# First layer's third branch as block-product pairs, in a one-core fp32 two-block network

## The chip, the core and the metric

The kernel runs on one core of a Trainium2 chip, everything in fp32. The metric is the device time of one execution in microseconds. TensorE (PE) multiplies, VectorE (DVE) and ScalarE (ACT) work on its results, SyncE (SP) issues the loads of weights, GpSimd (POOL) does little here.

## The reference, cut to what matters

A first block (RWKV-7 and S5 mixers, a convolutional feed-forward) is followed by a second block of two layers of width 1024. In its first layer (l = 0) 512 tokens are computed, 256 of the sequence and 256 of a context; in the second (l = 1) 256. In each layer three branches are gated and summed:

```
parts = split(h @ w_in + b_in)
y_a, yc_a = _gla_mixer(...)            # gated linear attention
y_b, yc_b = _mla_mixer(...)            # 8 softmax heads over 512 keys, then @ mla_wo
# third branch
h = a * sigmoid(g)                     # from parts[9]
h = depthwise_conv(h, 31 taps)
h = silu(layer_norm(h, g, b))
y_c = h @ conv_wo
# merge
g_a, g_b, g_c = split(sigmoid(parts[10]), 3)
y = (g_a * y_a + g_b * y_b + g_c * y_c) @ w_out
x = layer_norm(DN_ALPHA * x + gate1 * y); then a convolutional feed-forward
```

## The kernel before, in words

Features lie on the 128 partitions and tokens along the free axis, so a projection to 128 output features is a *job*: 8 matmuls (128x128 weights, 512 or 256 token columns) into one PSUM bank. Each fp32 matmul stands in the trace as two records. The order of the work is written out by hand: each engine has its own function per stage (`t_` TensorE, `a_` ScalarE, `v_` VectorE), its instructions run in the order written, and named steps (semaphores) tie the engines together. So whatever an engine waits for holds back all that is written behind it.

**Pairs.** `t_pair` (line 724; its matmuls are recorded on line 618) computes two output blocks at once, a 2x2 by 2x2 block product in seven products instead of eight (Winograd's form). Each product is 4 matmuls over half the token columns, 28 matmuls for a pair, in the order P1, P5, P6, a, P7, c, b. Around it VectorE makes four sums of weight blocks ahead (`v_block_sums` through `pair_sums`, lines 631 to 636: S1 is needed by P5, S2 by P6, S3 by P7, S4 by c), and four sums of the input, once for an input (`v_turns`, lines 771 to 776). ScalarE copies P1, P5, P6 and P7 out of PSUM (`a_pair_part`, line 790); P6 may start only when P1 has been copied, P7 when P6 has, c when P5 has, b when P7 has. A copy also waits until VectorE has read the same part of the pair before (the part of P1 is read by its step C11). VectorE adds the parts up (`v_pair_parts`, lines 802 and 808: C11, C22, C12).

**Weights.** All weights are streamed in one order, that of TensorE's use, in slabs of 8 tiles (512 KB, issued on line 4378) through a ring of 6 slabs. Slab s is loaded once slab s-6 is released. A job over 8 tiles releases its slab when its last matmul is done; a pair takes two slabs and releases both only at its end; a piece of the modulation (`more_ada`, line 1812, 8 matmuls with 32 of the tiles) takes four slabs and releases all four at its end.

**The first layer's third branch** (`t_branch_c`, `a_branch_c`, `v_branch_c`, `v_ln`): on TensorE two gate jobs, a piece of the modulation, the mean of the convolution's norm (line 3613), three gate jobs, the variance (line 3627), three gate jobs, two output jobs, and then three pairs `("cp", 0, m)` for the other six outputs. ScalarE takes the sigmoid of each gate straight out of PSUM (line 3603), the squares (3634), the root (3646, 3648) and the silu (3600); VectorE centres (3655), adds up the squares (3640), normalises (3664), sums the input for the pairs, and multiplies and adds the outputs into `Y`. The second branch before it (`t_branch_1`) is made of seven pairs already, the output projection after it (`t_wout`) of two jobs and three pairs.

**The attention's heads** (`t_mla`, `a_mla`, `v_mla`): per head and tile of 128 queries, scores (3329, 3330), maximum on VectorE (3346, 3348), exponential on ScalarE (3356), then ScalarE divides by the sum (`a_mla_norm`: logarithm 3364, exponential 3366, multiplication 3368), TensorE transposes two tiles later (3374), VectorE or ScalarE copies the result (3395, 3386), and TensorE multiplies by the values (3405). VectorE does the convolution's taps (3571) in between. Two gates of the second branch are computed inside the last head, and ScalarE takes their sigmoid (2896) there, with a load of its function table before and one back after it.

Of the kernel before, what the change touches and what calls it, by code (L numbers as in the profile page):

```python
# [17 lines left out]
P = 128  # L18
# [6 lines left out]
D = 1024  # L25
DT = D // P
TX = 256
# [225 lines left out]
def build(nc, t_in, out, known):  # L253
# [3 lines left out]
    with ctx:  # L257
# [271 lines left out]
        mo_tmp = area(mla_at + 11264, 1, 2, 512)[:, 0]  # L529
        assert s5_top <= total - 1024, (rw_top, s5_top)  # L530
# [2407 lines left out]
        def v_branch_1(l, n, done):  # L2938
# [38 lines left out]

        def v_branch_c(l, n):

            g, hn = mix_pairs[l], n // 2  # L2980
# [5 lines left out]
            for i, m in enumerate((2, 4, 6)):  # L2986
                pair_sums(g, i + 1)
                key = ("cp", l, m)

                def gated(e, c):  # L2990
                    cols = slice(c * hn, (c + 1) * hn)
                    ve.wait_ge(vector_steps, V.n)
                    ve.tensor_tensor(gct[:, e, cols], gct[:, e, cols], gtc[:, m + e, cols], ALU.mult).then_inc(vector_steps, V.step())

                v_pair_parts(g, key, lambda e, c: gct[:, e, c * hn:(c + 1) * hn], then=gated)
                ve.wait_ge(vector_steps, V.n)
                ve.tensor_tensor(Y[:, m, 0:n], Y[:, m, 0:n], gct[:, 0, 0:n], ALU.add).then_inc(vector_steps, V.step(("Y", l, 2, m)))
                ve.wait_ge(tensor_jobs, at(("job", (key, "b"))))
                ve.tensor_tensor(gct[:, 1, 0:hn], bank((key, "b"))[:, 0:hn], gtc[:, m + 1, 0:hn], ALU.mult).then_inc(vector_steps, V.step(("free", (key, "b"))))
                ve.wait_ge(vector_steps, V.n)  # L3000
                ve.tensor_tensor(Y[:, m + 1, 0:n], Y[:, m + 1, 0:n], gct[:, 1, 0:n], ALU.add).then_inc(vector_steps, V.step(("Y", l, 2, m + 1)))
# [367 lines left out]

        def t_mla_pt(l, n, hd, qt, k0):  # L3370
            pe.wait_ge(scalar_steps, at(("pn", l, hd, qt)))
# [112 lines left out]
        def v_mla(l, n):  # L3484
# [104 lines left out]

        def a_branch_c(l, n):  # L3590
            act.wait_ge(vector_steps, at(("free", ("br2", l, 1, DT - 1))))
# [566 lines left out]
        def _(tensor):  # L4158
# [39 lines left out]
            for l in range(LAYERS):  # L4198
# [13 lines left out]
                t_branch_c(l, n)  # L4212
# [8 lines left out]
        def _(scalar):  # L4221
# [25 lines left out]
            for l in range(LAYERS):  # L4247
# [18 lines left out]
                a_branch_c(l, n)  # L4266
# [10 lines left out]
        def _(vector):  # L4277
# [40 lines left out]
            for l in range(LAYERS):  # L4318
# [15 lines left out]
                v_ln(("cl", l), acc, n)  # L4334
                v_branch_c(l, n)
# [145 lines left out]
```

## Time and profile before

| | |
|---|---|
| median of 3 runs | 2681.27 us (2681.12 to 2682.8) |
| the profiled execution | 2679.76 us, of which the span of the trace is 2677.6 us |
| TensorE busy | 2622.1 us of the span |
| VectorE, ScalarE, GpSimd busy | 1825.7, 842.1, 86.1 us |
| mean granted TensorE clock | 0.995 |
| weights and inputs read | 309.81 MB, 116 GB/s over the span |

The profile is one execution; busy time counts records, start to end. In a timeline a row joins records of one line that follow each other. The span of the trace leaves 2.2 us of the execution's own time outside.

### The profile page before, as it was taken

The numbers are of one execution on the slowest core, as the hardware profiler recorded it, in microseconds if no ns is written. First come the engines' busy times: TensorE is split into PE (matmuls) and PEld (weight loads), VectorE is DVE, ScalarE is ACT, GpSimd is POOL, SyncE is SP. The second block draws the span as 40 slices with busy tenths as digits, with TensorE's granted clock in tenths as the row PEclk, the third lists the DMA queues.
The fourth block names the chain that finished last, engine by engine and source line by source line (L and its number), as shares of the span: only waits on it lengthen the run. The fifth ranks groups of instructions, "written<-read, shape, count | busy, mean of one in ns | idle before, by whom it ended". The sixth has DMA issues, their size and how long they took to land. (4 is left out here: it accounts for less than half of the span.)

```text
span 2677.6 us, 43472 instructions
## 1 busy us (share of the span) xinstructions
PE 2622.1 (98%) x17092; PEld 2191.1 (82%) x17092; DVE 1825.7 (68%) x3710; ACT 842.1 (31%) x1881; POOL 86.1 (3%) x115
## 2 busy tenths in 40 slices
PE   9999999999999999999999999999999999999998
PEld 8777799978776887668667888888798986798997
DVE  7882399644787477897647766644466557668997
ACT  2033143042543112552122423200454224333431
POOL 0000000001221000000000000000011000000000
PEclk9999999999999999999999999999999999999999
DMA  5553644433332222212322222222321441244443
GB/s 209 181 190 123 218 157 167 174 115 106 116 134 71 95 79 87 71 63 73 117 78 91 98 79 95 79 95 95 116 79 49 150 133 58 94 150 142 160 172 126
DMA packets 86776, 313.66 MB, mean 117 GB/s; under 512 B 9472, under 2 KB 11520, under 8 KB 86320
## 3 DMA queue, kind: packets, MB, share of 16 engines
q1 hardware_dynamic: 85072, 304.25, 32.5%
q0 software_dynamic: 1504, 6.64, 0.7%
q8 instruction: 138, 2.26, 0.3%
q14 instruction: 62, 0.51, 0.1%
HBM read 309.81 MB, written 1.05 MB: 116 GB/s over the span
## 5 line engine op out<-in xcount | busy, mean ns | idle before, releaser
L618 PE MATMUL ps<-sb 128*128 128x128 f32 (+1 forms) x8064 | 1292.9, 323 | 5.9 <-ACT sb L694 3.3
L618 PEld LDWEIGHTS ps<-sb 128*128 128x128 f32 x8064 | 1191.6, 191 | 108.9 <-issue 6.0
L921 PE MATMUL ps<-sb 128*128 128x256 f32 (+1 forms) x2480 | 681.6, 432 | 10.6 <-DVE sb L1000 3.5
L921 PEld LDWEIGHTS ps<-sb 128*128 128x128 f32 x2480 | 469.3, 190 | 207.8 <-issue 139.3
L3571 DVE SCALAR_TENSOR_TENSOR sb<-sb 128x512 f32<-128x512 f32 (+1 forms) x480 | 275.5, 615 | 8.7
L631 DVE TENSOR_TENSOR sb<-sb 128x512 f32<-128x512 f32 x155 | 106.3, 686 | 126.6 <-PE ps L618 85.6
L790 ACT COPY sb<-ps 128x256 f32<-128x256 f32 (+1 forms) x201 | 69.1, 344 | 391.9 <-PE ps L618 319.6
L694 ACT COPY sb<-ps 128x128 f32<-128x128 f32 (+1 forms) x252 | 75.3, 299 | 217.9 <-PE ps L618 213.0
L4142 DVE SCALAR_TENSOR_TENSOR sb<-sb 128x512 f32<-128x512 f32 (+1 forms) x176 | 101.0, 615 | 14.9 <-ACT sb L4088 9.9
L633 DVE TENSOR_TENSOR sb<-sb 128x512 f32<-128x512 f32 x155 | 107.2, 692 | 5.3
L808 DVE TENSOR_TENSOR sb<-sb,ps 128x256 f32<-128x256 f32 (+1 forms) x108 | 41.4, 384 | 98.6 <-PE ps L618 68.9
L636 DVE TENSOR_TENSOR sb<-sb 128x512 f32<-128x512 f32 x155 | 105.9, 683 | 0.0
L634 DVE TENSOR_TENSOR sb<-sb 128x512 f32<-128x512 f32 x155 | 105.9, 683 | 0.0
L727 PE MATMUL ps<-sb 128*128 128x128 f32 x896 | 100.7, 275 | 0.0
L727 PEld LDWEIGHTS ps<-sb 128*128 128x128 f32 x896 | 100.6, 192 | 0.1
L3753 ACT ACTIVATE sb<-sb 128x256 f32<-128x256 f32 (+1 forms) x28 | 12.8, 507 | 166.4 <-DVE sb L3830 152.0
L802 DVE TENSOR_TENSOR sb<-sb 128x256 f32<-128x256 f32 (+1 forms) x56 | 21.8, 390 | 51.3 <-ACT sb L790 43.2
L1812 PE MATMUL ps<-sb 128*32 128x512 f32 x384 | 51.7, 607 | 4.6 <-DMA sb<-in_w 4.6
L4088 ACT ACTIVATE sb<-sb 128x512 f32<-128x512 f32 (+1 forms) x84 | 54.9, 702 | 0.2
L2674 POOL TENSOR_TENSOR sb<-sb 128x256 f32<-128x256 f32 x56 | 47.7, 890 | 215.0 <-ACT sb L2602 215.0
L1000 DVE SCALAR_TENSOR_TENSOR sb<-sb 128x256 f32<-128x256 f32 x32 | 14.0, 479 | 48.8 <-ACT sb L982 38.2
L3346 DVE TENSOR_REDUCE sb<-ps 128x1 f32<-128x512 f32 (+1 forms) x48 | 28.7, 598 | 26.1 <-PE ps L3330 25.9
(518 smaller groups left out, 2761.9 us busy)
## 6 DMA issues: line engine op xcount, KB each, us to landing
sb<-in_w SPq DMA_DIRECT2D x574, 512.0 KB, 3.8
sb<-in_two POOLq DMA_DIRECT2D x2, 1088.0 KB, 7.3
sb<-in_x SPq DMA_DIRECT2D x2, 512.0 KB, 4.8
sb<-in_ctx POOLq DMA_DIRECT2D x1, 1024.0 KB, 9.7
sb<-in_v_bias POOLq DMA_DIRECT2D x2, 512.0 KB, 4.0
sb<-in_par SPq DMA_DIRECT2D x1, 764.0 KB, 6.6
sb<-in_s5b POOLq DMA_DIRECT2D x1, 512.0 KB, 7.9
sb<-in_s5c POOLq DMA_DIRECT2D x1, 512.0 KB, 9.9
```

What stands on the lines that cost most here:

```text
L618: ins = pe.matmul(o, w, xs(i), start=(fresh and i == 0), stop=(i == len(ws) - 1), skip_group_check=True)
L631: ve.tensor_tensor(buf[:, 0], half(s2, 0), half(s2, 1), ALU.add).then_inc(vector_steps, V.step(("S1", key)))
L633: ve.tensor_tensor(buf[:, 1], buf[:, 0], half(s1, 0), ALU.subtract).then_inc(vector_steps, V.step(("S2", key)))
L634: ve.tensor_tensor(half(s2, 0), half(s1, 0), half(s2, 0), ALU.subtract).then_inc(vector_steps, V.step(("S3", key)))
L636: ve.tensor_tensor(buf[:, 2], half(s1, 1), buf[:, 1], ALU.subtract).then_inc(vector_steps, V.step(("S4", key)))
L694: act.copy(f.part[:, i, :], bank((key, bk))[:, 0:f.hn]).then_inc(scalar_steps, A.step((name, key)))
L727: ins = pe.matmul(o[:, tt * P:(tt + 1) * P], xs(i)[:, tt * P:(tt + 1) * P], w, start=(fresh and i == 0 and tt == 0), stop=(i == len(ws) - ...
L790: act.copy(dst, src).then_inc(scalar_steps, A.step((name, key)))
L921: ins = pe.matmul(o[:, i * n:(i + 1) * n], w, rhs(k), start=(k == 0), stop=(k == kt - 1))
L3571: ve.scalar_tensor_tensor(out=o_, in0=s_, scalar=pc(("conv_dw", l, j), m + e), in1=o_, op0=ALU.mult, op1=ALU.add).then_inc(vector_steps, V ...
L4088: act.activation(zb2[e][:, g, 0:n].rearrange("p (a b) -> p a b", b=TX), z2[e][:, g, 0:c, 1:TX + 1], ACT.Identity, bias=pc(("ffn_db", l), g ...
L4142: ve.scalar_tensor_tensor(out=o_, in0=z2[e][:, g, 0:c, j:j + TX], scalar=pc(("ffn_dw", l, j), g * FT + m), in1=o_, op0=ALU.mult, op1=ALU.a ...
```

## The change

In the first layer the third branch's eight gates become four pairs (`cg_pairs`, on the same input sums as the second branch's gates), and its first two outputs become a pair, so that the branch is eight pairs. The mean of the norm stands behind the first of them, the variance behind the second, the piece of the modulation between the third and the fourth. Gates are written to SBUF without their sigmoid, which ScalarE takes later. In the heads, the two gates' sigmoids are put behind the divisions of the last head in both layers, and in the second layer the division moves from ScalarE to VectorE (a reciprocal and a multiplication), without the explicit table load ahead of the heads. The core of the diff:

```diff
+        cg_pairs = Pairs(TX, [area(mla_at + 12800 + i * 1536, 3, 4, P) for i in range(2)], parts_at(mla_at + 15872, TX),
+                         [("cg", 0, m) for m in (0, 2, 4, 6)] + [("cp", 0, 0)])
...
                 pair_sums(g, i + 1)
+                if i == len(g.seq) - 1:
+                    pair_sums(cg_pairs, 0)
...
+        def v_cg_parts(l, n, m):
+            hn = n // 2
+            v_pair_parts(cg_pairs, ("cg", l, m), lambda e, c: gtc[:, m + e, c * hn:(c + 1) * hn])
+
+        def v_branch_c_first(l, n):
+
+            tag, last = ("cl", l), cg_pairs.seq[-1]
+            pair_sums(cg_pairs, 1)
+            v_cg_parts(l, n, 0)
+            ve.wait_ge(tensor_jobs, at(("job", (tag, "mean"))))
+            for k in range(DT):
+                ve.scalar_tensor_tensor(out=acc(k)[:, 0:n], in0=bank((tag, "mean"))[:, 0:n], scalar=-1.0 / D, in1=acc(k)[:, 0:n],
+                                        op0=ALU.mult, op1=ALU.add).then_inc(vector_steps, V.step((tag, "cen", k)))
+            table[("free", (tag, "mean"))] = table[(tag, "cen", DT - 1)]
+            for k in range(1, DT):
+                ve.wait_ge(scalar_steps, at((tag, "sq", k)))
+                ve.wait_ge(vector_steps, V.n)
+                ve.tensor_tensor(lnS[:, 0:n], lnS[:, 0:n], cl_squares[k], ALU.add).then_inc(vector_steps, V.step((tag, "sqsum")))
+            pair_sums(cg_pairs, 2)
+            v_cg_parts(l, n, 2)
+            pair_sums(cg_pairs, 3)
+            ve.wait_ge(scalar_steps, at((tag, "rs")))
+            for k in range(DT):
+                ve.tensor_tensor(acc(k)[:, 0:n], acc(k)[:, 0:n], lnS[:, 0:n], ALU.mult).then_inc(vector_steps, V.step((tag, "nrm", k)))
+            v_cg_parts(l, n, 4)
+            pair_sums(cg_pairs, 4)
+            for k in range(DT):
+                ve.wait_ge(scalar_steps, at(("csilu", l, k)))
+            v_turns(conv_src[l])
+            v_cg_parts(l, n, 6)
+            ve.wait_ge(tensor_jobs, at(("job", (("cg", l, 6), "b"))))
+            pair_sums(mix_pairs[l], 0)
+            v_conv_pair(l, n, cg_pairs, 0)
+            for i, m in enumerate((2, 4, 6)):
+                pair_sums(mix_pairs[l], i + 1)
...
+        def v_mla_norm(l, n, hd, qt, k0):
+            s = spare_of(n, hd, qt)
+            ve.wait_ge(scalar_steps, at(("ex", l, hd, qt)))
+            ve.reciprocal(smx[:, s, 3:4], smx[:, s, 2:3]).then_inc(vector_steps, V.step())
+            ve.wait_ge(vector_steps, V.n)
+            ve.tensor_scalar(pr[s][:, k0:512], pr[s][:, k0:512], smx[:, s, 3:4], None, ALU.mult).then_inc(vector_steps, V.step(("pn", l, hd, qt)))
+
         def t_mla_pt(l, n, hd, qt, k0):
-            pe.wait_ge(scalar_steps, at(("pn", l, hd, qt)))
+            pe.wait_ge(*step_of(("pn", l, hd, qt)))
...
         def a_mla(l, n):
             (a_mla_in_first if l == 0 else a_mla_in)(l, n)
             parts = dict(qn=a_mla_qn, kn=a_mla_kn, vh=a_mla_vh, qr=a_mla_qr, qrs=lambda *x: None)
-            both_tables()
+            if l == 0:
+                both_tables()
...
                     old = later(n, hd, qt, 2)
                     if hd < MH:
                         a_mla_exp(l, n, hd, qt, k0)
-                    if (hd, qt) in gates_at(n):
-                        a_gate(l, n, 1, gates_at(n).index((hd, qt)), gtm)
-                        if hd < MH:
-                            both_tables()
                     if old is not None:
                         a_mla_pt(l, n, *old, qtiles(n)[old[1]][1])
-                    if hd < MH:
+                    if hd < MH and l == 0:
                         a_mla_norm(l, n, hd, qt, k0)
+                    if (hd, qt) == (MH - 1, n // P - 1):
+                        a_gate(l, n, 1, 0, gtm)
+                    if (hd, qt) == (MH, 1):
+                        a_gate(l, n, 1, 1, gtm)
...
+                    old = later(n, hd, qt, 1)
+                    if l and old is not None:
+                        v_mla_norm(l, n, *old, qtiles(n)[old[1]][1])
...
+        def t_branch_c_first(l, n):
+
+            for key in cg_pairs.seq:
+                kind, _, m = key
+                if kind == "cp":
+                    t_pair(cg_pairs, key, conv_src[l], "conv_wo_2", l, 0, P, ready=("csilu", l, DT - 1), first=True)
+                    continue
+                if m == 6:
+                    more_ada()
+                c = IN0["gate"] + 2 * D + m * P
+                t_pair(cg_pairs, key, head_src, "w_in_2", l, c, c + P)
+                if m == 0:
+                    t_ln_mean(("cl", l), n)
+                if m == 2:
+                    t_ln_var(("cl", l), n)
+            for m in (2, 4, 6):
+                t_pair(mix_pairs[l], ("cp", l, m), conv_src[l], "conv_wo_2", l, m * P, (m + 1) * P)
+
         def t_branch_c(l, n):
 
             for m in range(DT):
                 if m == 2:
-                    if l == 0:
-                        more_ada()
                     t_ln_mean(("cl", l), n)
...
+        def a_cg_parts(l, m, parts):
+            for i in parts:
+                a_pair_part(cg_pairs, ("cg", l, m), i)
+
+        def a_cg_close(l, n, m):
+            key = ("cg", l, m)
+            act.wait_ge(tensor_jobs, at(("job", (key, "b"))))
+            act.copy(gtc[:, m + 1, 0:n // 2], bank((key, "b"))[:, 0:n // 2]).then_inc(scalar_steps, A.step(("free", (key, "b"))))
...
+        def a_cl_silu(l, n, ks):
+            for k in ks:
+                act.wait_ge(vector_steps, at((("cl", l), "nrm", k)))
...
+        def a_branch_c_first(l, n):
+
+            tag, last = ("cl", l), cg_pairs.seq[-1]
+            a_cg_parts(l, 0, range(4))
+            a_cg_close(l, n, 0)
+            a_cl_squares(tag, (0, 1))
+            a_cg_parts(l, 2, (0,))
+            a_cl_squares(tag, (2, 3, 4))
+            a_cg_parts(l, 2, (1,))
+            a_cl_squares(tag, (5, 6, 7))
+            a_cg_parts(l, 2, (2, 3))
+            a_cg_close(l, n, 2)
+            a_ln_rs(tag, n)
+            a_cg_parts(l, 4, range(4))
+            a_cg_close(l, n, 4)
+            a_cl_silu(l, n, range(4))
+            a_cg_parts(l, 6, (0,))
+            a_cl_silu(l, n, (4, 5))
+            a_cg_parts(l, 6, (1,))
+            a_cl_silu(l, n, (6, 7))
+            a_cg_parts(l, 6, (2, 3))
+            a_cg_close(l, n, 6)
+            a_cg_sigmoid(l, n, (0,))
+            a_pair_part(cg_pairs, last, 0)
...
+            a_cg_sigmoid(l, n, (6, 7))
+            for m in (2, 4, 6):
+                for i in range(4):
+                    a_pair_part(mix_pairs[l], ("cp", l, m), i)
+
         def a_branch_c(l, n):
-            act.wait_ge(vector_steps, at(("free", ("br2", l, 1, DT - 1))))
...
-                v_ln(("cl", l), acc, n)
-                v_branch_c(l, n)
+                if l == 0:
+                    v_branch_c_first(l, n)
+                else:
+                    v_ln(("cl", l), acc, n)
+                    v_branch_c(l, n)
```

The former body of the loop in `v_branch_c` is now the function `v_conv_pair`, which for l = 0 also waits for the gate's sigmoid.

## Rows read from the trace of the kernel before

**Rows 1.** The page, part 1: busy time, share of the span, instructions.

```profile
PE 2622.1 (98%) x17092; PEld 2191.1 (82%) x17092; DVE 1825.7 (68%) x3710; ACT 842.1 (31%) x1881; POOL 86.1 (3%) x115
```

**Rows 2.** PE timeline, first layer's third branch: start us, us, instructions, xrecords.

```profile
1304.83 13.90 PE L921 MATMUL ps<-sb 128*128 128x512 f32 x32
1318.66 1.92 PE L1812 MATMUL ps<-sb 128*32 128x512 f32 x16
1320.51 1.12 PE L3613 MATMUL ps<-sb 128*128 128x512 f32 x2
1321.47 20.76 PE L921 MATMUL ps<-sb 128*128 128x512 f32 x48
1342.08 1.02 PE L3627 MATMUL ps<-sb 128*128 128x512 f32 x2
1342.93 34.50 PE L921 MATMUL ps<-sb 128*128 128x512 f32 x80
1377.27 36.42 PE L618 MATMUL ps<-sb 128*128 128x256 f32 x168
1413.53 13.90 PE L921 MATMUL ps<-sb 128*128 128x512 f32 x32
```

**Rows 3.** DVE timeline of the same stretch; in brackets the idle time before.

```profile
1321.75 2.48 DVE L3655 SCALAR_TENSOR_TENSOR sb<-ps,sb 128x512 f32<-128x512 f32 x4 [10.39 <-PE ps L3613]
...
1345.66 4.90 DVE L3664 TENSOR_TENSOR sb<-sb 128x512 f32<-128x512 f32 x8 [7.49 <-ACT sb L3648]
1364.84 0.42 DVE L771 TENSOR_TENSOR sb<-sb 128x256 f32<-128x256 f32 x1 [14.28 <-ACT sb L3600]
...
1370.70 0.68 DVE L631 TENSOR_TENSOR sb<-sb 128x512 f32<-128x512 f32 x1
...
1373.23 0.68 DVE L3011 TENSOR_TENSOR sb<-ps,sb 128x512 f32<-128x512 f32 x1
...
1384.44 0.42 DVE L808 TENSOR_TENSOR sb<-sb,ps 128x256 f32<-128x256 f32 x1 [2.84 <-PE ps L618]
...
1406.42 0.69 DVE L631 TENSOR_TENSOR sb<-sb 128x512 f32<-128x512 f32 x1 [3.63 <-DMA sb<-in_w]
```

**Rows 4.** ACT timeline of the same stretch.

```profile
1358.87 5.74 ACT L3600 ACTIVATE sb<-sb 128x512 f32<-128x512 f32 x8
...
1379.19 0.37 ACT L790 COPY sb<-ps 128x256 f32<-128x256 f32 x1 [12.58 <-PE ps L618]
```

**Rows 5.** Three windows: us, busy us (xrecords) by engine, PEclk, DMA share, GB/s.

```profile
2447.10:2450.15 3.05, 0.00 (x2) 0.03 (x1) 2.58 (x8) 1.56 (x4) 0.00 (x0) 1.00 0.00 1
2450.15:2454.10 3.95, 3.95 (x11) 3.18 (x12) 3.38 (x18) 3.68 (x7) 0.00 (x0) 0.57 0.00 0
1205.00:1210.00 5.00, 4.52 (x22) 3.85 (x23) 2.06 (x7) 3.50 (x11) 0.00 (x0) 1.00 0.01 3
```

**Rows 6.** PE timeline, then ACT timeline: end of the first layer's heads.

```profile
1202.95 0.60 PE L3374 MATMUL ps<-sb 128*128 128x128 f32 x4
1205.48 2.83 PE L3405 MATMUL ps<-sb 128*128 128x256 f32 x12 [1.92 <-DVE sb L3571]
...
1201.71 1.28 ACT L2896 ACT_TABLE_LOAD   x1
...
1205.00 0.37 ACT L3386 COPY sb<-ps 128x256 f32<-128x256 f32 x1
```

**Rows 7.** PE timeline, then ACT timeline: start of the second layer's heads.

```profile
2222.67 1.95 PE L3277 MATMUL ps<-sb 128*128 128x128 f32 x16
2225.19 1.12 PE L3329 MATMUL ps<-sb 128*128 128x512 f32 x2 [0.57 <-ACT sb L3300]
...
2224.57 0.57 ACT L3300 COPY sb<-ps 128x512 f32<-128x512 f32 x1
```

**Rows 8.** Window of two heads of the second layer; DVE timeline, multiplication by a scalar.

```profile
2230.03:2253.53 23.50, 23.50 (x110) 16.66 (x109) 18.94 (x42) 8.22 (x23) 0.00 (x0) 1.00 0.17 54
...
1420.23 2.77 DVE L3826 TENSOR_SCALAR sb<-sb 128x512 f32<-128x512 f32 x8
```

More of the change, by code:

```diff
@@ L529, in build @@
         mo_tmp = area(mla_at + 11264, 1, 2, 512)[:, 0]
+        cg_pairs = Pairs(TX, [area(mla_at + 12800 + i * 1536, 3, 4, P) for i in range(2)], parts_at(mla_at + 15872, TX),
+                         [("cg", 0, m) for m in (0, 2, 4, 6)] + [("cp", 0, 0)])
+        cl_squares = [lnS, lnq[:, 0], lnq[:, 1]] + [sb[:, mla_at + 4096 + i * 512:mla_at + 4608 + i * 512] for i in range(4)] + [gtc[:, DT - 1]]
         assert s5_top <= total - 1024, (rw_top, s5_top)
@@ L2976, in v_some_taps @@
             return min(done + more, 4 * CW)
+        def v_cg_parts(l, n, m):
[31 more added lines that the diff above has]
+                pair_sums(mix_pairs[l], i + 1)
+                v_conv_pair(l, n, mix_pairs[l], m)
@@ new lines, in v_conv_pair, with gated @@
+        def v_conv_pair(l, n, g, m):
+            key, hn = ("cp", l, m), n // 2
+            def gated(e, c):
+                cols = slice(c * hn, (c + 1) * hn)
+                if l == 0:
+                    ve.wait_ge(scalar_steps, at(("gates2", l, m + e)))
+                ve.wait_ge(vector_steps, V.n)
+                ve.tensor_tensor(gct[:, e, cols], gct[:, e, cols], gtc[:, m + e, cols], ALU.mult).then_inc(vector_steps, V.step())
+            v_pair_parts(g, key, lambda e, c: gct[:, e, c * hn:(c + 1) * hn], then=gated)
+            ve.wait_ge(vector_steps, V.n)
+            ve.tensor_tensor(Y[:, m, 0:n], Y[:, m, 0:n], gct[:, 0, 0:n], ALU.add).then_inc(vector_steps, V.step(("Y", l, 2, m)))
+            ve.wait_ge(tensor_jobs, at(("job", (key, "b"))))
+            ve.tensor_tensor(gct[:, 1, 0:hn], bank((key, "b"))[:, 0:hn], gtc[:, m + 1, 0:hn], ALU.mult).then_inc(vector_steps, V.step(("free", (key, "b"))))
+            ve.wait_ge(vector_steps, V.n)
+            ve.tensor_tensor(Y[:, m + 1, 0:n], Y[:, m + 1, 0:n], gct[:, 1, 0:n], ALU.add).then_inc(vector_steps, V.step(("Y", l, 2, m + 1)))
@@ L2978, in v_branch_c @@
         def v_branch_c(l, n):
-            g, hn = mix_pairs[l], n // 2
+            g = mix_pairs[l]
             for k in range(DT):
@@ L2987, in v_branch_c @@
                 pair_sums(g, i + 1)
[L2988 to L3001, printed above, removed]
+                v_conv_pair(l, n, g, m)
         def v_branch(l, n, b, gbuf, tbuf, stop=DT):
@@ L3368, in a_mla_norm @@
             act.activation(pr[s][:, k0:512], pr[s][:, k0:512], ACT.Identity, scale=smx[:, s, 3:4]).then_inc(scalar_steps, A.step(("pn", l, hd, qt)))
+        def v_mla_norm(l, n, hd, qt, k0):
+            s = spare_of(n, hd, qt)
+            ve.wait_ge(scalar_steps, at(("ex", l, hd, qt)))
+            ve.reciprocal(smx[:, s, 3:4], smx[:, s, 2:3]).then_inc(vector_steps, V.step())
+            ve.wait_ge(vector_steps, V.n)
+            ve.tensor_scalar(pr[s][:, k0:512], pr[s][:, k0:512], smx[:, s, 3:4], None, ALU.mult).then_inc(vector_steps, V.step(("pn", l, hd, qt)))
         def t_mla_pt(l, n, hd, qt, k0):
-            pe.wait_ge(scalar_steps, at(("pn", l, hd, qt)))
+            pe.wait_ge(*step_of(("pn", l, hd, qt)))
             o = open_job(("pt", l, hd, qt))
@@ new lines, in a_cl_squares @@
+        def a_cl_squares(tag, ks):
+            for k in ks:
+                act.wait_ge(vector_steps, at((tag, "cen", k)))
+                act.activation(cl_squares[k], acc(k), ACT.Square).then_inc(scalar_steps, A.step((tag, "sq", k)))
+        def a_cl_silu(l, n, ks):
+            for k in ks:
+                act.wait_ge(vector_steps, at((("cl", l), "nrm", k)))
+                act.activation(acc(k)[:, 0:n], acc(k)[:, 0:n], ACT.Silu, bias=pc(("conv_ln_b", l), k),
+                               scale=pc(("conv_ln_g", l), k)).then_inc(scalar_steps, A.step(("csilu", l, k)))
@@ new lines, in a_cg_sigmoid @@
+        def a_cg_sigmoid(l, n, ms):
+            for m in ms:
+                act.wait_ge(vector_steps, at(("C12", ("cg", l, m - m % 2))))
+                act.activation(gtc[:, m, 0:n], gtc[:, m, 0:n], ACT.Sigmoid, bias=pc(("b_in", l, "gate"), 2 * DT + m)).then_inc(scalar_steps, A.step(("gates2", l, m)))
+        def a_branch_c_first(l, n):
[21 more added lines that the diff above has]
+            a_pair_part(cg_pairs, last, 0)
+            a_cg_sigmoid(l, n, (1, 2))
+            a_pair_part(cg_pairs, last, 1)
+            a_cg_sigmoid(l, n, (3,))
+            a_pair_part(cg_pairs, last, 2)
+            a_cg_sigmoid(l, n, (4, 5))
+            a_pair_part(cg_pairs, last, 3)
+            a_cg_sigmoid(l, n, (6, 7))
+            for m in (2, 4, 6):
+                for i in range(4):
+                    a_pair_part(mix_pairs[l], ("cp", l, m), i)
@@ L4211, in _ @@
                     t_branch(l, n, 1, "mla_wo_2", lambda k: mO[:, k, 0:n], ahead=GATES_AHEAD)
-                t_branch_c(l, n)
+                (t_branch_c_first if l == 0 else t_branch_c)(l, n)
                 t_wout(l, n)
@@ L4265, in _ @@
                     a_branch(l, n, 1, gtm, first=2)
-                a_branch_c(l, n)
+                (a_branch_c_first if l == 0 else a_branch_c)(l, n)
                 for m in (2, 4, 6):
@@ L4333, in _ @@
                     v_ln_sum(("cl", l), acc, n, k)
-                v_ln(("cl", l), acc, n)
-                v_branch_c(l, n)
+                if l == 0:
+                    v_branch_c_first(l, n)
+                else:
+                    v_ln(("cl", l), acc, n)
+                    v_branch_c(l, n)
                 v_ln_close(l, n, "wo2", 2, ("l1", l), ("ln1_g", l), ("ln1_b", l), (l, 1))
```

## The prediction

> **What bounds the kernel now.** First the page's busy times: TensorE is busy for 98% of the span [rows 1], so time is to be had from its records or from its few waits. Then TensorE's timeline of the branch: from the first gate job at 1304.83 to the end of the last pair at 1413.53 one row starts where the last one ends, 108.70 us without a wait, and no row has a bracket of idle time [rows 2]. VectorE's and ScalarE's timelines of the same stretch show what stands behind each wait: VectorE was idle for 7.49 us before its normalisation and 14.28 us before the input sums [rows 3]. So here only TensorE's amount of work counts, until another engine is late. Last come the heads, where TensorE does wait for ScalarE [rows 6, 7].
>
> **TensorE's work.** The three pairs took 1413.53 - 1377.27 = 36.26 us, 12.09 each, 0.432 per matmul of 256 columns [rows 2]. Ten jobs become five pairs. The jobs took 1318.66 - 1304.83 = 13.83 (two), 1342.08 - 1321.47 = 20.61 (three) and 1377.27 - 1342.93 = 34.34 (five), together 68.78. Five pairs are 60.43. That is **-8.35 us**, all on the path. Modulation (1320.51 - 1318.66 = 1.85), mean and variance are the same work elsewhere. Ten slabs stay ten slabs.
>
> **What the other engines add.** VectorE gets five times four weight sums, 2.53 a pair (from the first 631 row at 1370.70 to 1373.23) [rows 3], and the adding up. That is some 18 us on top of 51 busy in 108.7 us; the sum fits, only the order can hurt. I went through the order, putting the pairs at 12.09. First pair (0 to 12.09): the sums for the second pair and the parts of the first are done before the mean is. Mean at 12.1: centring eight times at 0.6 (four took 2.48), then seven sums of squares at about 0.7, each behind the one before (the 512-column records) [rows 3], end about 11 us later; the variance is due at 25.0 and is ready at 23.3. Root: ready two microseconds before the third pair needs ScalarE. No stall up to the end of the third pair, which I call E.
>
> **The stall.** Between third and fourth pair stands the modulation, moved here with its four slabs. The fourth pair's two slabs are the fifth and sixth behind the third pair's end, so in a ring of 6 they take the places of exactly the third pair's two slabs, released at E and not before. The trace has that case: the pair ending at 1377.27 + 24.17 = 1401.44 releases two slabs, and the weight sums that need them start at 1406.42 behind a wait for DMA: 4.98 us [rows 3]. There it cost nothing, as the pair was due only 12 us later. Here TensorE is due after 1.85. And behind the fourth pair's weight sums VectorE has queued the whole normalisation and the third pair's parts; behind these ScalarE has the silus and the copy of the fourth pair's P1 (it waits for C11 of the third). So from E: slabs 4.98; weight sums 2.53 to 7.51; eight multiplications, 4.83 start to start (4.90 took the row) to 12.34 [rows 3]; C11 0.42 [rows 3]; hand over 0.09; copy 0.37 [rows 4]; hand over 0.11 (the two hand-overs from neighbouring ends and starts in these timelines): **13.33**. P6 would have started at 1.85 + 8 matmuls of 0.432 = 5.30. Stall **+8.03 us**, in two pieces: some 2 us for the first slab and S1, then 5.8 us idle before P6. After P6 nothing is late: ScalarE's four silus left, 0.72 each (eight in 5.74 [rows 4]), and two copies take 3.9 us, as long as P6 and the next product. The input sums of the convolution, 5.86 us (1364.84 to 1370.70) [rows 3], end 22.2 behind E, and the fifth pair wants them at 23.7. From there all runs as before. If the landing is 1 us longer or shorter, so is the stall.
>
> **The clock.** Before the record at 2450.15 TensorE had been idle for 3.05 us; in the 3.95 us behind it the granted clock is 0.57, full and half clock (2.4 and 1.2 GHz) mixed: 0.43 x 3.95 = 1.7 us lost. Behind an idle piece of 1.92 us it is 1.00 [rows 5, 6]. 5.8 us idle is longer than either. Bounds: zero (as behind the shorter wait) and 3.4 (the stretch at half clock twice as long); a gain is excluded. I take the nearest row, **+1.7**. The Trainium skill (TensorE: Matmul & The Clock Gate, Part 1) says that the half clock is the default and activity releases it, so that a long wait is followed by a full cold stretch each time; by that the cost leans to the upper bound. No row has an idle piece as long in mid-work to show it.
>
> **The heads, first layer.** Sigmoid of the first gate, with a table load before it and another behind (1201.71 to 1205.00), delays the copy at 1205.00, for which TensorE waits 1.92 us at 1205.48 [rows 6]. Put behind the last division, the sigmoid leaves the copy free right after the transposes, well before TensorE asks. What is late next is the gate's own bank, wanted about 1214, its sigmoid then done about 1211.5. **-1.9**.
>
> **The heads, second layer.** TensorE waits 0.57 us at 2225.19 for a copy that ScalarE reaches at 2224.57 [rows 7] behind three division steps, 1.1 us of which go to VectorE. **-0.6**. The table load that was explicit now comes by itself ahead of the first exponential, while ScalarE waits. VectorE gets 16 times a reciprocal of one column and a multiplication over 512: the latter between 0.42 (the row of eight at 1420.23, whose records are that long) [rows 8] and 0.69 (a 512-column tensor operation [rows 3]), the reciprocal by the one-column ScalarE steps some 0.2; I take 0.75 together. Two heads have 18.94 busy of 23.50 us [rows 8]; four times 0.75 makes 21.9. Cost nothing, covered by the matmuls; if the cover is gone, up to 0.75 x 16 = 12 us.
>
> **Sum:** -8.35 + 8.03 + 1.7 - 1.9 - 0.6 = -1.1 us on the profiled execution of 2679.76, so 2678.6; the median stands 1.5 above that execution, so **2680.1 us**. No change that a measurement can tell: that takes about 0.2%, 5.4 us.
>
> **Rivals.**
> 1. *The wait is covered.* The slabs come in time, or VectorE is not held by them. Then 2681.27 - 8.35 - 2.5 = 2670.4; with TensorE waiting only for landing and S1 (2.2 us), 2672.6. For it: the branch shows no wait before, and the modulation is easy to misplace by a slab. Against it: ring arithmetic and the 4.98 us [rows 3]. Chance 0.15.
> 2. *Half clock twice as long*, by the idle piece of 5.8 us: 2680.1 + 1.7 = 2681.8. The Trainium skill's page above leans this way. Chance 0.17.
> 3. *Slower: VectorE becomes the bound in the second layer's heads.* Place: 16 divisions queued ahead of the taps, each also waiting for the exponential. Two heads leave 4.56 us, 1.14 a division [rows 8]; beyond that every further 0.5 us costs 8. At 1.64 us: 2680.1 + 0.6 + 8 = 2688.7. Against it: the prices above, half of that. Chance 0.06.
> 4. *The change saves no TensorE time*, 28 small matmuls costing what 16 wide ones do: 2680.1 + 8.35 = 2688.5. Against it: the three pairs measured beside it [rows 2]. Chance 0.02.
>
> The forecast itself has 0.60. Its own range: favourable ends (no clock loss, landing 1 us shorter) 2677.4, the others (clock 3.4, landing longer, heads give nothing) 2685.3. To leave out no more than 2 in 10 I go from 2674.5 to 2684.5. Faster by over 0.2% is rival 1: 0.15, plus 0.01 of a much shorter stall, 0.16; slower 3 and 4, 0.08; the rest, 0.76, within.
>
> **What would show it.** The branch's TensorE rows: eight pairs of 12.1 us; up to E no bracket; behind the modulation an idle piece of about 2 us (DMA or line 631), then one of about 5.8 before the third product of the fourth pair, put down to ScalarE's copy; VectorE idle some 13 us before the sums (line 631) of the fourth pair, waiting for in_w; PEclk below 1 behind it. At the first layer's last head the 1.92 us gone. It would be wrong if no such wait shows and the branch takes 100 us, or if the second layer's heads take longer than the 11.75 us each (23.50 for two) [rows 8].

## The result, and the profile after

The changed kernel is **slower** by 0.2%: a median of 2687.39 us over 13 runs (2682.87 to 2691.32), against 2681.27 over 13 runs of the kernel before (2679.87 to 2684.28) beside them. The ratio is 1.0021 with a 95% interval of 1.0014 to 1.0029. 2680.1 us was forecast, within 2674.5 to 2684.5. The miss is 7.3 us and its sign was given a chance of 0.08. (One run of f1 below took 3911.89 us at a mean granted clock of 0.65; it counts in the median of five but not in the ratio, and the other four lie between 2668.74 and 2670.34.)

Part 1 of the page, after:

```profile
PE 2620.9 (97%) x17212; PEld 2218.6 (82%) x17212; DVE 1852.8 (69%) x3779; ACT 825.8 (31%) x1852; POOL 86.0 (3%) x115
```

Against [rows 1], TensorE works 1.2 us less in 120 records more, where the plan has 8.35 us less work. A span of 2689.2 us with less busy time means idle time, and busy time that shrinks by less than the work means a slower clock somewhere. So I went down TensorE's timeline from where the change begins. The profiled execution took 2691.32 us, the longest of the 13. It was 6.33 us behind the trace of before at the transposes of the first layer's last head (1209.28 against 1202.95), upstream of everything that was changed. The clock makes up part of that: after, the granted clock is 0.91, 0.86 and 0.93 over 205 to 225, 265 to 290 and 325 to 350 us, where before it is 1.00 throughout; before it is 0.91 and 0.94 over 660 to 680 and 700 to 730 us, where after it is 1.00. One minus the clock, times the length, gives 7.0 against 3.6 us, an estimate from above, as idle time lies in these windows. So nothing below rests on differences of spans; I compare stages, each from its own first record.

TensorE's timeline, end of the first layer's heads (start us, us, line, operation, xrecords, idle time before and what ended it):

```profile
1209.28 0.60 PE L3429 MATMUL ps<-sb 128*128 128x128 f32 x4
1209.71 2.76 PE L3460 MATMUL ps<-sb 128*128 128x256 f32 x12
1212.30 0.59 PE L3377 MATMUL ps<-sb 128*128 128x256 f32 x2
1212.74 0.59 PE L3378 MATMUL ps<-sb 128*128 128x256 f32 x2
1213.17 0.60 PE L3429 MATMUL ps<-sb 128*128 128x128 f32 x4
1218.04 8.83 PE L924 MATMUL ps<-sb 128*128 128x512 f32 x16 [4.27 <-ACT sb L2899]
1226.70 0.60 PE L3429 MATMUL ps<-sb 128*128 128x128 f32 x4
1227.87 2.83 PE L3460 MATMUL ps<-sb 128*128 128x256 f32 x12 [0.56 <-DVE sb L3450]
```

ScalarE's timeline of the same stretch:

```profile
1208.66 0.37 ACT L3441 COPY sb<-ps 128x256 f32<-128x256 f32 x1 [0.65 <-PE ps L3429]
...
1216.00 1.28 ACT L2899 ACT_TABLE_LOAD   x1
1217.29 0.69 ACT L2899 ACTIVATE sb<-ps,sb 128x512 f32<-128x512 f32 x1
```

The 1.92 us wait of [rows 6] is gone: the copy at 1208.66 follows its transposes, and the product at 1209.71 carries no bracket. But the second gate's matmuls (line 924, due at 1213.60) now wait 4.27 us for the *first* gate's sigmoid (line 2899). That sigmoid stands behind all divisions of the last head and starts at 1217.29; 0.75 us later the matmuls start. They then take 8.83 us, where the 16 records of the first gate, at 1201.32, took 7.03 us.

TensorE's timeline of the third branch, from the mean that lies behind its first pair:

```profile
1327.22 1.02 PE L3747 MATMUL ps<-sb 128*128 128x512 f32 x2
1328.08 12.25 PE L621 MATMUL ps<-sb 128*128 128x256 f32 x56
1340.17 1.02 PE L3761 MATMUL ps<-sb 128*128 128x512 f32 x2
1341.03 12.25 PE L621 MATMUL ps<-sb 128*128 128x256 f32 x56
1353.21 1.92 PE L1815 MATMUL ps<-sb 128*32 128x512 f32 x16
1356.95 4.01 PE L621 MATMUL ps<-sb 128*128 128x256 f32 x16 [1.82 <-DMA sb<-in_w]
1366.57 60.21 PE L621 MATMUL ps<-sb 128*128 128x256 f32 x264 [5.62 <-ACT sb L793]
1426.62 13.90 PE L924 MATMUL ps<-sb 128*128 128x512 f32 x32
```

VectorE's timeline behind the modulation, then ScalarE's:

```profile
1358.20 0.69 DVE L634 TENSOR_TENSOR sb<-sb 128x512 f32<-128x512 f32 x1 [15.58 <-issue]
...
1360.74 4.90 DVE L3006 TENSOR_TENSOR sb<-sb 128x512 f32<-128x512 f32 x8
1365.55 0.41 DVE L811 TENSOR_TENSOR sb<-sb,ps 128x256 f32<-128x256 f32 x1
```

```profile
1353.70 1.28 ACT L3682 ACT_TABLE_LOAD   x1
1361.46 2.93 ACT L3682 ACTIVATE sb<-sb 128x512 f32<-128x512 f32 x4 [6.47 <-DVE sb L3006]
1366.06 0.37 ACT L793 COPY sb<-ps 128x256 f32<-128x256 f32 x1 [1.67 <-DVE sb L811]
```

This is the forecast chain, link by link: VectorE idle for 15.58 us, four weight sums (from 1358.20), the eight multiplications of the normalisation, C11 (line 811), the copy at 1366.06, TensorE at 1366.57. "issue" is a wait that the profile can't name; TensorE's bracket of 1.82 names the slab, in_w. The first of the four sums, S1, ends at 1358.89, and the weights of the fourth pair's second product (P5) are loaded right behind it. TensorE's weight loads (PEld):

```profile
1358.96 1.59 PEld L621 LDWEIGHTS ps<-sb 128*128 128x128 f32 x8 [0.42 <-issue]
```

Windows around the two long waits (us, busy us of PE, PEld, DVE, ACT, POOL with xrecords, granted clock, DMA share, GB/s):

```profile
1213.60:1218.04 4.44, 0.17 (x3) 0.01 (x1) 4.34 (x6) 4.29 (x10) 0.00 (x0) 1.00 0.00 0
1218.04:1226.70 8.66, 8.66 (x16) 3.68 (x17) 0.73 (x1) 0.00 (x0) 0.00 (x0) 0.80 0.20 61
1360.75:1366.57 5.82, 0.21 (x1) 0.03 (x1) 5.82 (x13) 3.44 (x6) 0.00 (x0) 0.93 0.36 144
1366.57:1374.00 7.43, 7.43 (x21) 6.06 (x22) 6.71 (x17) 3.32 (x6) 0.00 (x0) 0.59 0.00 0
```

Behind each the granted clock is a mixture of 2.4 and 1.2 GHz, 0.80 and 0.59: 0.20 x 8.66 = 1.7 us and 0.41 x 7.43 = 3.0 us lost.

The second layer's heads take 2322.17 - 2227.09 = 95.08 us from the first head's transposes to the last product's start (before: 2310.93 - 2214.44 = 96.49). The product that waited 0.57 us [rows 7] has no bracket now:

```profile
2235.32 1.95 PE L3325 MATMUL ps<-sb 128*128 128x128 f32 x16
2237.10 1.02 PE L3377 MATMUL ps<-sb 128*128 128x512 f32 x2
```

Stage by stage on TensorE:

| stage | before | after | difference | forecast |
|---|---|---|---|---|
| transposes of the first layer's last head to the first pair of branch 1 | 17.27 | 21.25 | **+3.98** | -1.9 |
| branch 1, seven pairs | 84.61 | 84.60 | 0 | 0 |
| third branch, first gate to end of last pair | 108.70 | 111.49 | **+2.79** | +1.4 |
| all behind it | 1264.07 | 1262.58 | **-1.49** | -0.6 |
| sum | | | **+5.28** | -1.1 |

After, branch 1 starts at 1230.53 and the third branch at 1315.13 (the mean's 1327.22 less one pair, 12.09). The measured difference of the medians is 6.12 us, so 0.8 us of it isn't in these stages.

### The profile page after: what moved, and what is told of

It is laid out like the page before. It is cut to its first block and busy times, and to the rows that moved or that the text cites. A ratio compares the mean times of both kernels' runs of the same rounds, so it can differ in the third digit from the quotient of the medians.

```text
span 2689.2 us, 43799 instructions
## 1 busy us (share of the span) xinstructions
PE 2620.9 (97%) x17212; PEld 2218.6 (82%) x17212; DVE 1852.8 (69%) x3779; ACT 825.8 (31%) x1852; POOL 86.0 (3%) x115
## 5 line engine op out<-in xcount | busy, mean ns | idle before, releaser
L621 PE MATMUL ps<-sb 128*128 128x128 f32 (+1 forms) x8344 | 1357.2, 325 | 13.0 <-ACT sb L793 6.0
L621 PEld LDWEIGHTS ps<-sb 128*128 128x128 f32 x8344 | 1246.7, 191 | 126.1 <-DVE sb L805 6.8
L924 PE MATMUL ps<-sb 128*128 128x256 f32 (+1 forms) x2320 | 618.8, 425 | 14.8 <-ACT sb L2899 4.3
L924 PEld LDWEIGHTS ps<-sb 128*128 128x128 f32 x2320 | 442.7, 192 | 176.9 <-issue 102.4
L634 DVE TENSOR_TENSOR sb<-sb 128x512 f32<-128x512 f32 x160 | 109.9, 687 | 142.8 <-PE ps L621 95.5
L793 ACT COPY sb<-ps 128x256 f32<-128x256 f32 (+1 forms) x221 | 76.3, 345 | 410.2 <-PE ps L621 342.7
L636 DVE TENSOR_TENSOR sb<-sb 128x512 f32<-128x512 f32 x160 | 110.7, 692 | 5.5
L637 DVE TENSOR_TENSOR sb<-sb 128x512 f32<-128x512 f32 x160 | 109.5, 684 | 0.0
L639 DVE TENSOR_TENSOR sb<-sb 128x512 f32<-128x512 f32 x160 | 109.4, 684 | 0.0
L730 PEld LDWEIGHTS ps<-sb 128*128 128x128 f32 x896 | 100.6, 192 | 0.1
L3404 ACT ACTIVATE sb<-ps,sb 128x512 f32<-128x512 f32 (+1 forms) x48 | 29.6, 617 | 53.5 <-DVE sb L3396 53.5
```

The lines of the kernel that those rows point to most:

```text
L621: ins = pe.matmul(o, w, xs(i), start=(fresh and i == 0), stop=(i == len(ws) - 1), skip_group_check=True)
L634: ve.tensor_tensor(buf[:, 0], half(s2, 0), half(s2, 1), ALU.add).then_inc(vector_steps, V.step(("S1", key)))
L636: ve.tensor_tensor(buf[:, 1], buf[:, 0], half(s1, 0), ALU.subtract).then_inc(vector_steps, V.step(("S2", key)))
L637: ve.tensor_tensor(half(s2, 0), half(s1, 0), half(s2, 0), ALU.subtract).then_inc(vector_steps, V.step(("S3", key)))
L639: ve.tensor_tensor(buf[:, 2], half(s1, 1), buf[:, 1], ALU.subtract).then_inc(vector_steps, V.step(("S4", key)))
L730: ins = pe.matmul(o[:, tt * P:(tt + 1) * P], xs(i)[:, tt * P:(tt + 1) * P], w, start=(fresh and i == 0 and tt == 0), stop=(i == len(ws) - ...
```

## The experiments

Each kernel is the changed one with one edit or several; the median stands beside runs of the kernel before on the same chip (2681.67, 2681.01 and 2681.18 us in the three batches). Runs of one kernel spread mostly over 4 to 9 us, so a difference of 2 us between medians says nothing by itself. The timelines decide where the time went; the medians say whether it was real.

### Whose wait is it at the second gate?

The theory now: a PSUM bank (TensorE writes each job into one of 8 banks, and the bank can be written again only once its reader is done). open_job hands out banks in turn and skips the held ones. The modulation's bank is held, so the turn has seven banks, and the second gate, seventh job behind the first, gets the first gate's bank. **e1_raw_copy** frees that bank early: the gate is copied out raw after the last head's second division, and its sigmoid is taken in place later.

```
+ if l == 0 and (hd, qt) == (MH - 1, 1):
+     act.wait_ge(tensor_jobs, at(("job", ("gt", l, 1, 0))))
+     act.copy(gtm[:, 0, 0:n], bank(("gt", l, 1, 0))[:, 0:n]).then_inc(scalar_steps, A.step(("free", ("gt", l, 1, 0))))
...
-     a_gate(l, n, 1, 0, gtm)
+     if l:
+         a_gate(l, n, 1, 0, gtm)
+     else:
+         act.wait_ge(scalar_steps, A.n)
+         act.activation(gtm[:, 0, 0:n], gtm[:, 0, 0:n], ACT.Sigmoid, bias=pc(("b_in", l, "gate"), DT)).then_inc(scalar_steps, A.step())
```

> The changed kernel, but in the first layer ScalarE copies gate 0 of the second branch raw out of PSUM right after the first division of the last head (no table load), and takes its sigmoid in SBUF at the place where the change has it. Theory (bank): of the 8 PSUM banks one is held for the modulation, so the jobs go round 7 banks, gate 1's job is the seventh after gate 0's and gets its bank, and TensorE waits 4.3 us for gate 0's sigmoid; the copy frees the bank before gate 1 is due, so this wait and the half-clock stretch behind it (1.8 us) go: 6 us less than the changed kernel, about 2681.3 us. Rival (ScalarE's load): the divisions are late by themselves; then the copy delays them by 0.6 us more, a wait of about 4 us stays before gate 1 or before the transposes, and the time stays within 1 us of 2687.4.

Measured: 2678.78 us (11 runs), ratio 0.9989 (0.998 to 0.9998). TensorE's timeline:

```profile
1204.49 0.60 PE L3429 MATMUL ps<-sb 128*128 128x128 f32 x4
1204.93 7.03 PE L924 MATMUL ps<-sb 128*128 128x512 f32 x16
```

No wait, and 7.03 instead of 8.83 us. From the transposes (1200.60) to branch 1 (1215.63) it is 15.03 us, 6.22 less than after and 2.24 less than before. The wait is the bank's, and both it and the half clock behind it are the change's.

A copy also changes when ScalarE is busy. **g1_next_bank** therefore touches ScalarE not at all: it moves TensorE on by one bank ahead of the second gate.

```
+ if l == 0 and hd == MH:
+     jobs[0] += 1
```

> The changed kernel with one line more on TensorE: in the first layer the PSUM bank whose turn it is is passed over before gate 1 of the second branch, so that gate 1 takes the bank after it; ScalarE and VectorE do exactly what they do in the changed kernel. Theory (the bank and nothing else): the wait of 4.3 us before gate 1 and its half-clock stretch (1.8 us) go, with gate 0's sigmoid as late as in the changed kernel: 2681.3. Rival (something else that ends at the same time as the sigmoid holds gate 1 back, the divisions or the input sums for the pairs): the wait stays, 2687.4.

Measured: 2678.24 us (10 runs), ratio 0.9987 (0.9977 to 0.9996). TensorE's timeline, then ScalarE's:

```profile
1209.89 7.03 PE L924 MATMUL ps<-sb 128*128 128x512 f32 x16
```

```profile
1213.58 0.69 ACT L2899 ACTIVATE sb<-ps,sb 128x512 f32<-128x512 f32 x1
```

The sigmoid comes as late as ever, 3.7 us *after* the second gate's matmuls have started, and nobody waits for it. Not the sigmoid's lateness costs time, but the bank that it holds. One line of TensorE's order, without a new instruction, brings this stage from 21.25 to 15.02 us, the same as the copy.

**f4_gates_back** undoes the part: the first layer's gate sigmoids go back inside the last head.

```
+ if l == 0 and (hd, qt) in gates_at(n):
+     a_gate(l, n, 1, gates_at(n).index((hd, qt)), gtm)
+     if hd < MH:
+         both_tables()
...
- if (hd, qt) == (MH - 1, n // P - 1):
+ if l and (hd, qt) == (MH - 1, n // P - 1):
...
- if (hd, qt) == (MH, 1):
+ if l and (hd, qt) == (MH, 1):
```

> The changed kernel with the first layer's two gate sigmoids put back inside the last head as before. Theory: the 1.92 us wait for the transposes' copy comes back, the 4.3 us wait before gate 1 and its half-clock stretch (1.8 us) go: 4.1 us less than the changed kernel, 2683.3. Rival (the place of the sigmoid does not matter): 2687.4.

Measured: 2682.52 us (11 runs), ratio 1.0006 (0.9997 to 1.0015). TensorE's timeline:

```profile
1206.76 2.83 PE L3460 MATMUL ps<-sb 128*128 128x256 f32 x12 [1.92 <-DVE sb L3634]
...
1210.72 7.03 PE L924 MATMUL ps<-sb 128*128 128x512 f32 x16
```

The old wait of 1.92 us is back, the new one is gone, and the stage takes 1221.51 - 1204.24 = 17.27 us, exactly that of before. The part as it was made costs 4.0 us by the trace (4.9 by the medians).

### What holds the fourth pair?

Three theories were open for the third branch: slabs only, VectorE's order, or ScalarE's. **e4_sums_late** moves the fourth pair's weight sums behind the normalisation and the third pair's parts in VectorE's queue; the slabs come no earlier.

```
- pair_sums(cg_pairs, 3)
  ve.wait_ge(scalar_steps, at((tag, "rs")))
...
  v_cg_parts(l, n, 4)
+ pair_sums(cg_pairs, 3)
  pair_sums(cg_pairs, 4)
```

> The changed kernel, but VectorE makes the weight sums of the fourth gate pair only after the normalisation and the third pair's parts; slabs and modulation stay where the change has them. Theory (it is the queue behind the sums that costs, the slabs alone only 2 us): TensorE still waits 1.8 us for the slab and a few tenths for S1 (line 634), then P6 starts on time; the 5.6 us and the half-clock stretch go: some 9 us less than the changed kernel, 2678.4. Rival (the slabs' landing itself costs the whole wait): the idle time before P6 stays over 4 us.

Measured: 2677.25 us (11 runs), ratio 0.9984 (0.9975 to 0.9992). TensorE's timeline, VectorE's, and a window over the 280 records (its last three numbers are granted clock, DMA share and GB/s):

```profile
1345.57 1.92 PE L1815 MATMUL ps<-sb 128*32 128x512 f32 x16
1349.28 61.25 PE L621 MATMUL ps<-sb 128*128 128x256 f32 x280 [1.78 <-DMA sb<-in_w]
```

```profile
1335.80 4.90 DVE L3005 TENSOR_TENSOR sb<-sb 128x512 f32<-128x512 f32 x8 [0.83 <-ACT sb L3782]
...
1350.54 0.69 DVE L634 TENSOR_TENSOR sb<-sb 128x512 f32<-128x512 f32 x1 [6.09 <-DMA sb<-in_w]
```

```profile
1349.28:1410.37 61.09, 61.01 (x280) 53.14 (x281) 37.96 (x77) 17.69 (x36) 0.00 (x0) 1.00 0.29 106
```

The normalisation now runs 9.7 us ahead of the third pair's end (1345.5) instead of 7.6 behind it. The wait of 5.62 us is gone; the slab's own, 1.78, is left. No half clock follows: it is 1.00 over all 280 records. Three quarters of the stall's idle time were work that was ready, queued behind a wait for data.

**e3_ada_in_heads** goes at the slabs: the modulation leaves the third branch for a third place in the heads, so that no slabs come between third and fourth pair.

```
- ADA_HEADS = (2, 5)
+ ADA_HEADS = (1, 3, 5)
- if m == 6:
-     more_ada()
```

> The changed kernel, but the piece of the modulation that stands before the fourth gate pair is computed inside the first layer's heads (three pieces there instead of two), so that no four slabs stand between the third and the fourth pair. Theory (slabs and queue order): the fourth pair's slabs are there long before; the idle pieces of 1.8 and 5.6 us and the half-clock stretch (3.3 us) go. A wait of 1.7 us before the fourth pair's P6 takes their place, because ScalarE takes four silus (2.9 us) before it copies P1: about 9.7 us less than the changed kernel, 2677.7. Rival (ScalarE's silus or VectorE's amount of work are the bound, not the slabs): the idle piece before P6 stays over 4 us and the time over 2682.

Measured: 2676.18 us (9 runs), ratio 0.9976 (0.9967 to 0.9986). TensorE's timeline:

```profile
1215.73 9.55 PE L924 MATMUL ps<-sb 128*128 128x512 f32 x16 [4.26 <-ACT sb L2899]
...
1339.44 15.70 PE L621 MATMUL ps<-sb 128*128 128x256 f32 x72
1356.74 57.22 PE L621 MATMUL ps<-sb 128*128 128x256 f32 x264 [1.59 <-ACT sb L793]
```

No wait for in_w; the fourth pair's slabs now take the place of the first pair's, free long before. Left is 1.59 us for ScalarE's copy, which stands behind silus. It also gives the clock's price cleanly: these 264 records take 57.22 us at full clock, and took 60.21 after, **2.99 us** more behind the 5.62 us wait.

### Together, and what each part is worth

**f1_all** has both repairs (raw copy, modulation in the heads) and starts the silus earlier, between the third pair's copies:

```
- a_cg_parts(l, 4, range(4))
+ a_cg_parts(l, 4, (0, 1, 2))
+ a_cl_silu(l, n, (0, 1, 2))
+ a_cg_parts(l, 4, (3,))
+ a_cl_silu(l, n, (3, 4, 5))
...
- a_cl_silu(l, n, range(4))
- a_cg_parts(l, 6, (0,))
- a_cl_silu(l, n, (4, 5))
- a_cg_parts(l, 6, (1,))
...
- a_cg_parts(l, 6, (2, 3))
+ a_cg_parts(l, 6, range(4))
```

> All three repairs together: gate 0 copied raw in the last head, the piece of the modulation in the heads, and ScalarE's silus started between the third pair's parts so that P1 of the fourth pair is copied on time. Theory: no idle piece is left from the last head's gates to the output projection, the third branch takes 8 x 12.09 + 1.7 for mean and variance = 98.4 us, and the sum of the single gains holds: 2687.4 - 6.1 - 8.1 - 3.3 = 2669.9 by the traces of the changed kernel, 0.4% less than the kernel before. Rival (the gains share a cause, such as half-clock stretches that fall elsewhere): over 2673.

Measured: 2670.24 us (five runs), ratio **0.9955** (0.9942 to 0.9969). TensorE's timeline:

```profile
1222.52 2.83 PE L3460 MATMUL ps<-sb 128*128 128x256 f32 x12 [0.56 <-DVE sb L3450]
1225.18 10.09 PE L621 MATMUL ps<-sb 128*128 128x256 f32 x46
...
1335.68 72.68 PE L621 MATMUL ps<-sb 128*128 128x256 f32 x336
1408.20 13.90 PE L924 MATMUL ps<-sb 128*128 128x512 f32 x32
```

The row of 336 records is six pairs without a gap. The branch takes 1408.20 - (1225.18 + 84.61) = 98.41 us: eight pairs of 12.09 plus mean and variance (0.86 each). This version beats both kernels.

**f2_raw_sums_late** joins e1's edit and e4's.

> Gate 0 copied raw, and the fourth pair's weight sums behind the normalisation, the modulation left where the change has it. Theory: 2.3 us more than the kernel with all repairs, which is the wait for the fourth pair's slabs alone: 2672.2. Rival (with the gates repaired the slabs' wait brings a half-clock stretch of its own): 1.7 us or more on top, 2674.

Measured: 2671.48 us (five runs), ratio 0.9963 (0.9951 to 0.9976). TensorE's timeline:

```profile
1343.00 62.39 PE L621 MATMUL ps<-sb 128*128 128x256 f32 x280 [1.92 <-DMA sb<-in_w]
```

The same 280 records and the same kind of wait as in e4, where they took 61.25 us in all; without any loss they would take 57.22 + 3.46 = 60.7. Here 1.7 us were lost behind 1.92 us idle, and the granted clock of the first four us (1343.00 to 1347.00) is 0.57. The 0.6 us of e4 are no clock, which is 1.00 there, but two pauses of some 0.3 us: the weight loads at 1351.30 (behind S1, which ends at 1351.23) and at 1363.65 carry brackets of 0.42 and 0.40. A short wait sometimes brings a half clock and sometimes none. The median lies 1.2 us above f1's; with runs from 2667.35 to 2675.62 that decides nothing.

**f3_old_branch** keeps the change's heads with the raw copy, and takes back the third branch: ten jobs as before, on VectorE too.

```
- (t_branch_c_first if l == 0 else t_branch_c)(l, n)
+ t_branch_c(l, n)
...
- (a_branch_c_first if l == 0 else a_branch_c)(l, n)
+ a_branch_c(l, n)
```

> The third branch as in the kernel before (eight gate jobs, two output jobs, three pairs), with the changed heads of both layers and gate 0 copied raw. Theory: what is left of the change without its pairs is the heads alone, -1.9 in the first layer and -1.4 in the second: 3.3 us less than the kernel before, 2678.4, and 8.5 us more than the kernel with all repairs. Rival (the pairs bring less than their matmuls): under 6 us more than that kernel.

Measured: 2677.85 us (11 runs), ratio 0.9984 (0.9976 to 0.9993); the branch takes 1413.92 - 1305.23 = 108.69 us, as before. f1 is 7.6 us below it, and the trace shows 108.69 - 98.41 = 10.28 us, 1.85 of it the modulation that f1 has in the heads, so 8.43 of TensorE's work. The pairs are worth what was forecast, once nothing waits.

**e5_l1_back** undoes the second layer's heads:

```
- if l == 0:
-     both_tables()
+ both_tables()
+ if l and (hd, qt) in gates_at(n):
+     a_gate(l, n, 1, gates_at(n).index((hd, qt)), gtm)
- if l and old is not None:
+ if l > 1 and old is not None:
```

> The changed kernel, but the second layer's heads are those of the kernel before: division on ScalarE, gates' sigmoids inside the last head, explicit table load. Theory (the second layer's edit gains by ScalarE being free earlier): its heads take 1.4 us longer again, the 0.57 us wait before the second head's scores comes back, 2688.8. Rival (VectorE's new work costs there): faster than the changed kernel. A difference this small will hardly show in the median; the profile decides.

Measured: 2685.78 us (11 runs), ratio 1.0014 (1.0005 to 1.0023). The median went down where it should go up by 1.4 us; between kernels that spread over 8 us it decides nothing. The timeline does: the heads take 2315.33 - 2218.84 = 96.49 us, that of before to the hundredth, and the old wait is there:

```profile
2229.60 1.12 PE L3377 MATMUL ps<-sb 128*128 128x512 f32 x2 [0.57 <-ACT sb L3348]
```

So by the trace this part is worth 1.41 us. That it is worth anything in the median is not shown.

Not tried: the modulation between the first layer's two output products of the heads. VectorE's sums for the first output pair are queued ahead of parts that TensorE would then have to deliver first, so each would wait for the other.

## Why the prediction was wrong

**The step that failed** is the term -1.9 of "The heads, first layer", and in it one sentence: "What is late next is the gate's own bank, wanted about 1214, its sigmoid then done about 1211.5." It named the right thing, and the sigmoid's end was right: it is 1217.29 + 0.69 = 1217.98 after, and 1211.65 in the time of before (6.33 less). Wrong was the moment at which the bank is wanted. The second gate's job is due right behind the last transposes, and these move forward with the 1.92 us that go: 1213.60 after, 1207.3 in the time of before. 1214 is about where that job ends. The turn of the banks was not counted: with one held there are seven, so the second gate itself is the next to want this one, which g1 shows. It cost 4.27 us idle and 1.8 us of clock where 1.9 were to be won; the stage came out at +3.98, a miss of 5.9 us, most of the 7.3. This miss alone takes the forecast of 2680.1 past the upper end of 2684.5; that of the clock alone, 1.3 us, would not have.

**The clock.** Taken 1.7 us, from the row behind 3.05 us idle. Measured behind 5.62 us: 2.99. e1, e5 and f4, which keep that wait, take 60.07 to 60.18 us for the same 264 records, against 57.22. That is nearer to rival 2 (3.4, at a chance of 0.17) than to the 1.7 taken. The 16 records ahead of that wait took 4.01 against 3.6 us, but at a granted clock of 1.00 (1356.95 to 1360.75): that is the wait for S1, and part of the stall. The Trainium skill (TensorE: Matmul & The Clock Gate, Part 1) says that the clock is halved by default and activity releases it. The trace agrees behind every wait of over 4 us in these kernels' heads and third branch, though not with the same cost each time: 1.8 us behind 4.27, 2.5 in e3 (9.55 against 7.03) behind 4.26. The nearest row was the wrong choice here, as the idle piece was nearly twice as long as that row's. Nor did that row stand for its own length: in the trace of before TensorE also waits 3.22 us, up to 270.81, and loses nothing behind it. TensorE's timeline, then a window:

```profile
270.81 27.89 PE L921 MATMUL ps<-sb 128*128 128x256 f32 x128 [3.22 <-DVE sb L1436]
```

```profile
270.81:280.81 10.00, 10.00 (x46) 8.84 (x47) 2.77 (x4) 0.00 (x0) 0.91 (x1) 1.00 0.96 341
```

**The stall** was right. The third product of the fourth pair was forecast at E + 13.33; E is the modulation's start less 0.08, 1353.13, and the row starts at 1366.57, at E + 13.44. The two idle pieces were forecast at 2 (slab and S1) and 5.8 us, and are 1.82, with 0.4 for S1 behind it, and 5.62. e3 and e4 show its two causes apart: without the slabs' late release the larger piece shrinks to 1.59 us, with the other order on VectorE it goes.

**TensorE's work**, -8.35: right. Two pairs of 56 records in 12.25 us each stand in the timeline, and f1 against f3 gives 7.6 us in the median. With the stall of 8.14 and the clock's 2.99 the branch comes to +2.78; +2.79 was measured.

**The second layer's heads**: -1.41 by the trace for -0.6. Some 0.8 goes at the first wait; the rest lies in three pieces of 0.1 us, one in every second head, and 0.26 us around the last gate, which the prediction had not listed. VectorE did not become the bound: rival 3's mechanism did not occur, though the sign that it stood for did. **Rival 1** (wait covered) did not occur, but f1 and f2 reach its time, 2670.4, with other orders. **Rival 4** is refuted by the pairs.

So the sum, term by term, is -8.35 + 8.14 + 2.99 + 3.98 - 1.41 = +5.35 us where -1.1 stood. The slower side was priced by a late VectorE in the second layer and by pairs that save nothing. A wait that takes the place of the removed one, in the same stage, had not been given a chance, though the text had come within one instant of it.

What stays open: e1 and g1 lie 8.6 and 9.1 us below the changed kernel's median, while their timelines show 6.2 us less in that stage. Part of the rest can be clock elsewhere. The mean granted clock over all runs is 0.9923 for the changed kernel (13 runs), 0.9937 for e1 (11), 0.9944 for g1 (10) and 0.9945 to 0.9947 for the kernel before in the three batches. Times 2687 us the differences of e1 and g1 are 3.8 and 5.6 us, an estimate from above, as time at half clock costs nothing while TensorE is idle; 1.8 of it lies in the stage. Where the other stretches at half clock fall differs between kernels whose work there is the same: over 265 to 290 us the clock is 0.86 after and 1.00 before. The records of the runs don't say where their clock was low, so what a wait costs on average stays open.

## What to carry to other kernels

When a consumer is moved back in its engine's queue, look for who next writes into the buffer that it reads: count the rotation by the buffers that are really free at that place, without the held ones, and put the *start* of that next job against the new end of the consumer, both in the same time. A releasing copy or a skipped buffer makes the lateness harmless, here for 0.6 us of ScalarE or for nothing. And when an in-order queue holds both work that is ready and a wait for a transfer, ready work goes first: that alone took away 5.6 us of stall and the half clock behind it.

## What was unexpected of the hardware

The half clock can cost nearly as much as a short wait itself, and is not fixed by the wait's length. Behind 1.78 us idle nothing was lost to the clock (e4), behind 1.92 us 1.7 (f2) and elsewhere nothing [rows 5, 6], behind 3.22 us nothing (before), behind 4.26 to 4.27 us 1.8 (after) and 2.5 (e3), behind 5.62 us 3.0. In g1 a stretch of it fell into the 16 records behind a wait of 1.95 us, 5.41 against 3.6 us, and 264 records behind 4.24 us took 58.91 against 57.22.

```profile
1347.14 5.41 PE L621 MATMUL ps<-sb 128*128 128x256 f32 x16 [1.95 <-DMA sb<-in_w]
1356.79 58.91 PE L621 MATMUL ps<-sb 128*128 128x256 f32 x264 [4.24 <-ACT sb L793]
```

Part of the spread shows in e3 and after. After, the clock is still 1.00 up to the end of the wait (1213.60 to 1218.04). In e3 it has fallen within the wait and stays low for longer, 0.77 over the wait and 0.74 over the gate's matmuls behind it; what falls into the wait costs nothing.

```profile
1211.47:1215.73 4.26, 0.00 (x0) 0.00 (x1) 4.16 (x6) 4.11 (x9) 0.00 (x0) 0.77 0.00 0
1215.73:1225.12 9.39, 9.39 (x17) 4.04 (x18) 0.73 (x1) 0.00 (x0) 0.00 (x0) 0.74 0.18 56
```

The table load ahead of the silus does not wait for their data: ScalarE loads at 1353.70 and then stands for 6.47 us before the first silu at 1361.46. A load that looks like part of a late step is paid for in idle time.
